# Attention over compressed blocks: high and low keys in one product of 64 columns, sums of two token tiles at once, score steps between the key features, two key banks kept in SBUF

## The chip, the cores and the metric

The kernel runs on one core of one Trainium2 chip. The core has five engines that share nothing but memory and semaphores: TensorE (PE in the rows; its weight loads are PEld), VectorE (DVE), ScalarE (ACT), GpSimd (POOL) and SyncE (SP), which issues the transfers. The metric is the device time of one execution in microseconds, the median of several runs. The inputs are float32; products are made either in float32 or with operands rounded to fp32r, a high part and a low part apart.

## The reference, cut to what matters

Two transformer blocks are computed for 512 tokens of width 1024. The change lies in the second one's mixer, which has 16 query heads of width 64 in 4 groups (heads of a group share keys), and three attentions that are gated and summed: over 31 compressed blocks of 32 tokens, over selected blocks, and over a window.

```python
q, kc, vc, ks, vs, kw, vw, gl = jnp.split(h @ w_in, cuts, axis=-1)
q = q.reshape(B, S, G, Hg, dk) * dk ** -0.5
gates = jax.nn.sigmoid(gl).reshape(B, S, G, Hg, 3)
k_cmp = _compress(kv(kc), pe_k, ck_w1, ck_w2)      # 31 compressed keys per group
v_cmp = _compress(kv(vc), pe_v, cv_w1, cv_w2)
...
p_cmp = masked_softmax(jnp.einsum('bghtd,bngd->bghtn', qg, k_cmp), cmp_end[None, :] <= t[:, None])
o_cmp = jnp.einsum('bghtn,bngd->btghd', p_cmp, v_cmp)
...
o = g_blk[..., 0:1] * o_cmp + g_blk[..., 1:2] * o_sel + g_blk[..., 2:3] * o_win
```

With 512 tokens all 8 selection blocks are taken, and the window covers all earlier tokens, so o_sel and o_win are two causal attentions with keys of their own.

## The kernel before

**Weights.** All projections go through one plan of weight tiles. SP loads them into a ring of six (`load_weights`, L322), ACT rounds each to its high part (`split_high`, L335, the copy is L344), POOL subtracts to get the low part (`split_low`, L347, L352), and PE makes three fp32r matmuls per block of 128 (`product`, L362: high times high, L365, and twice high times low, L366 and L367). ACT may round a tile only when PE has used the third tile before it, and SP may load one when POOL has made the low part of the sixth before it. Every engine runs its own list in the order of the code; engines meet at semaphores (`wait_ge`, `then_inc`).

**The stage around the change** starts at L2195. PE makes in turn: keys and values for compression, the 16 heads' queries (`nq`: rows 0 to 63 hold a head's high part, rows 64 to 127 its low part), the compression network, the token-major values (`values_of`; c=1 leaves them in PSUM banks 0 to 3, c=0 in banks 4 and 5), and four products with key features (`feature(k_at + i, i)`, 24 matmuls of 512 columns each, into banks 0 to 3). The attention over the compressed blocks is spread between these, for four token tiles t of 128 tokens:

- `block_scores(t)` (PE, L2287): for each of 16 heads two matmuls of 32 columns, one with the high and one with the low compressed keys `kcmp[0]`, `kcmp[1]`, into bank 6 + t % 2;
- `soften(t)` (DVE, L2456): mask added, row maximum, maximum subtracted; `block_exp(t)` (ACT, L2378); `norm_blocks(t)` (DVE, L2467): sum, reciprocal, gate, multiplied;
- `block_turn(t)` (PE, L2298): four transposes into the same bank; `block_copy(t)` (ACT, L2382) copies them to `cpT`;
- `block_values(t)` (PE, L2305): eight float32 products of 128 columns with `vcmp`, into banks 4 and 5 whatever t is; `finish(t)` (DVE, L2479) copies the sums to `oT`.

PE's order in the key features (L2346 to L2360): feature 0, turn 0, feature 1, values 0, scores 2, feature 2, turn 1, values 1, feature 3, scores 3, turn 2, values 2, turn 3, values 3.

**Keys.** When the four key features are in their banks, ACT copies 8 parts of 64 rows by 512 to `hT` (`key_high`), DVE makes the low parts (`key_low`), and SP copies each from rows 0 to 63 to rows 64 to 127 (L2561, four transfers per group, semaphore `k_twice[g]`).

**The next stage** ("pairs", L2566) runs 64 steps of two heads each over the four groups, the tiles and the two key sets: PE scores (L2600 to L2602), DVE maximum (L2688), ACT exponential (L2672), POOL reciprocal (L2720) and scaling (L2722), PE transposes (L2612), ACT and DVE high and low copies, PE values (L2627 to L2631), DVE sums into `oT`. PE makes the scores of the first step and then waits for `c_done`, that is for `finish(3)`; POOL's first step stands behind its last `split_low` of the stage before.

## Time and profile before

| what | value |
|---|---|
| median of 3 runs | 1810.1 us (1809.75 to 1811.23) |
| the profiled execution | 1811.46 us, its span 1809.7 us |
| PE busy | 1738.3 us, 96% of the span |
| DVE, ACT, POOL busy | 53%, 46%, 53% |
| mean granted TensorE clock | 0.981 |
| share of the last chain | PE 40%, DVE 5%, issue 2%, ACT 2%, POOL 1% |

The span runs from the first to the last instruction; 1.8 us of the execution lie around it. A granted clock of 1.00 is 2.4 GHz and 0.50 is 1.2 GHz. The stage of the change spans about 902 to 1078 us, the pairs 1078 to 1222 us. In a timeline row the first number is the start, the second the length; "x16" means that 16 instructions are merged; in square brackets stands the idle time of the engine before it and what ended that. Matmul ends are modelled, so the distance between two starts is the better measure of what one costs.

### The profile page before, as it was taken

Reading aid. Unit: us, or ns where it says so; the run is one execution under the profiler, and the core shown is the slowest. Engines: PE = TensorE matmul, PEld = TensorE weight load, DVE = VectorE, ACT = ScalarE, POOL = GpSimd, SP = SyncE. Lnnn points to the kernel's source line nnn. Section 1 sums busy time; section 2 is a strip of 40 time slices with the busy share of each in tenths; the row PEclk is TensorE's granted clock in tenths of the full one; section 3 lists DMA queues with packets and bytes.
Section 4 is the critical chain, followed back from the end, with each engine's and each line's share of the span. In section 5 each row is a group of like instructions: output and inputs, shape, how many; then the busy total and the mean of one; then the engine's idle time right before and its main releaser. Section 6 shows DMA issues by size and latency. Waiting matters only on the chain.

```text
span 1809.7 us, 27577 instructions
## 1 busy us (share of the span) xinstructions
PE 1738.3 (96%) x10430; PEld 1540.8 (85%) x10430; DVE 965.4 (53%) x1638; ACT 833.1 (46%) x1659; POOL 953.4 (53%) x697
## 2 busy tenths in 40 slices
PE   6999999999999999999899989999899999999998
PEld 4998887888878998999778978887788779989996
DVE  2246555353638742772346449994224388618842
ACT  4224543232335542553445238884434356516643
POOL 2454342344535764775346328992652358647852
PEclk9999999999999999999999979999999989999999
DMA  6232221123342332333235130012341223323331
GB/s 229 82 94 59 58 72 50 53 74 94 96 163 78 110 115 83 94 117 117 81 98 151 64 93 2 2 36 70 120 137 66 63 70 117 112 87 94 106 129 47
DMA packets 222901, 162.09 MB, mean 90 GB/s; under 512 B 9769, under 2 KB 197297, under 8 KB 222769
## 3 DMA queue, kind: packets, MB, share of 16 engines
q1 hardware_dynamic: 221712, 159.26, 28.8%
q8 instruction: 84, 1.38, 0.3%
q10 hardware_dynamic: 1056, 1.06, 0.2%
q14 instruction: 49, 0.39, 0.1%
HBM read 156.09 MB, written 2.11 MB: 87 GB/s over the span
## 4 chain that ended last, share of the span: by engine, by line
PE 40%; DVE 5%; issue 2%; ACT 2%; POOL 1%; DVEq 0%; ACTq 0%
PE psum L365 12%; PE psum L366 12%; PE psum L367 12%; DVE nprobL L2695 2%; DVE stat L2688 1%; PE psum L2612 1%; PE psum L2294 1%; POOL w_low L352 1%; PE psum L2628 0%; DVE oT L2704 0%; PE psum L2312 0%; PE psum L2627 0%; PE psum L449 0%; PE psum L2600 0%; ACT w_high L344 0%
## 5 line engine op out<-in xcount | busy, mean ns | idle before, releaser
L352 POOL TENSOR_TENSOR w_low<-ring,w_high 128x1024 fp32r<-128x1024 f32 (+2 forms) x223 | 483.4, 2172 | 633.0 <-ACT w_high L344 632.4
L365 PE MATMUL psum<-hT,w_high 128*128 128x512 f32 (+1 forms) x1072 | 377.5, 352 | 9.5 <-PEq L184 6.4
L344 ACT ACTIVATE w_high<-ring 128x1024 fp32r<-128x1024 f32 (+2 forms) x223 | 212.1, 954 | 375.3 <-PE psum L367 375.2
L366 PE MATMUL psum<-hL,w_high 128*128 128x512 f32 (+1 forms) x1072 | 371.4, 346 | 0.0
L367 PE MATMUL psum<-hT,w_low 128*128 128x512 f32 (+1 forms) x1072 | 371.1, 346 | 0.0
L365 PEld LDWEIGHTS psum<-hT,w_high 128*128 128x128 f32 x1072 | 206.9, 193 | 32.8 <-issue 6.6
L367 PEld LDWEIGHTS psum<-hT,w_low 128*128 128x128 f32 x1072 | 206.4, 193 | 24.9
L366 PEld LDWEIGHTS psum<-hL,w_high 128*128 128x128 f32 x1072 | 206.8, 193 | 21.8
L1784 POOL TENSOR_TENSOR w_low<-ffn_sums,w_high 128x512 fp32r<-128x512 f32 x120 | 169.1, 1423 | 51.1 <-ACT w_high L1779 50.8
L1784 POOL TENSOR_TENSOR w_low<-ring,w_high 128x512 fp32r<-128x512 f32 x120 | 155.1, 1294 | 60.7 <-ACT w_high L1779 53.9
L365 PE MATMUL psum<-ffn_th,w_high 128*128 128x256 f32 x640 | 181.6, 284 | 4.9 <-DVE ffn_g L2018 3.3
L367 PE MATMUL psum<-ffn_th,w_low 128*128 128x256 f32 x640 | 181.4, 283 | 0.0
L366 PE MATMUL psum<-ffn_tl,w_high 128*128 128x256 f32 x640 | 181.3, 283 | 0.0
L752 DVE TENSOR_TENSOR x<-x,psum 128x512 f32<-128x512 f32 x56 | 36.0, 683 | 230.2 <-PE psum L367 230.2
L365 PE MATMUL psum<-w_high,ffn_act 128*128 128x512 f32 x352 | 137.2, 390 | 0.0
L366 PE MATMUL psum<-w_low,ffn_act 128*128 128x512 f32 x352 | 137.0, 389 | 0.0
L367 PE MATMUL psum<-w_high,ffn_act 128*128 128x512 f32 x352 | 136.9, 389 | 0.0
L365 PEld LDWEIGHTS psum<-ffn_th,w_high 128*128 128x128 f32 x640 | 123.0, 192 | 5.5 <-DVE ffn_g L2018 3.7
L367 PEld LDWEIGHTS psum<-ffn_th,w_low 128*128 128x128 f32 x640 | 123.1, 192 | 0.0
L366 PEld LDWEIGHTS psum<-ffn_tl,w_high 128*128 128x128 f32 x640 | 123.0, 192 | 0.0
L365 PE MATMUL psum<-w_high,hT 128*128 128x256 f32 (+2 forms) x320 | 106.2, 332 | 3.6 <-POOL w_low L352 2.9
L1779 ACT ACTIVATE w_high<-ring 128x512 fp32r<-128x512 f32 x120 | 75.2, 630 | 73.2 <-PE psum L367 73.1
(436 smaller groups left out, 3775.8 us busy)
## 6 DMA issues: line engine op xcount, KB each, us to landing
ring<-in_w_in SPq DMA_DIRECT2D x58, 512.0 KB, 3.4
ring<-in_ffn_w_up SPq DMA_DIRECT2D x44, 512.0 KB, 3.8
ring<-in_w_gate SPq DMA_DIRECT2D x22, 512.0 KB, 3.7
ring<-in_w_up SPq DMA_DIRECT2D x22, 512.0 KB, 4.7
ring<-in_w_down SPq DMA_DIRECT2D x20, 512.0 KB, 3.7
ring<-in_ffn_w_down SPq DMA_DIRECT2D x20, 512.0 KB, 3.9
ring<-in_nsa_w_in SPq DMA_DIRECT2D x18, 512.0 KB, 3.5
ring<-in_ca_wkv SPq DMA_DIRECT2D x16, 512.0 KB, 3.6
```

What stands on the lines that cost most here:

```text
L344: nc.scalar.activation(tile_view(w_high, n, SPLIT), tile_view(ring, n, RING), ACT.Copy).then_inc(w_hi, 1)
L352: nc.gpsimd.tensor_tensor(tile_view(w_low, n, SPLIT), tile_view(ring, n, RING), tile_view(w_high, n, SPLIT), ALU.subtract).then_inc(w_lo, 1)
L365: nc.tensor.matmul(ps, lhsT=sh, rhs=mh, start=first, stop=False)
L366: nc.tensor.matmul(ps, lhsT=sh, rhs=ml_, start=False, stop=False)
L367: return nc.tensor.matmul(ps, lhsT=sl, rhs=mh, start=False, stop=last)
L752: return nc.vector.tensor_tensor(dst, dst, ps, ALU.add)
L1779: nc.scalar.activation(operand_place(w_high, r, j), self.source(r, name), ACT.Copy).then_inc(u_high, 1)
L1784: nc.gpsimd.tensor_tensor(operand_place(w_low, r, j), self.source(r, name), operand_place(w_high, r, j), ALU.subtract).then_inc(u_low, 1)
L2294: mm = nc.tensor.matmul(bank[6 + t % 2][:, 32 * h:32 * h + 32], lhsT=nq[:, h, q_tile(t)], rhs=kcmp[k][:, h // HPG, :], start=(k == 0), sto ...
L2612: mm = nc.tensor.transpose(bank[4 + v_ % 2][:, j * P:(j + 1) * P], nprob[:, v_ % 8, j * P:(j + 1) * P], ident)
L2688: nc.vector.tensor_reduce(np_peak[s % 2], psum[:, 2 * (s % 2):2 * (s % 2) + 2, 0:wd], AXX, ALU.max, negate=True).then_inc(p_peaked, 1)
L2695: nc.vector.tensor_tensor(nprobL[:, v_ % 4, 0:(t + 1) * P], bank[4 + v_ % 2][:, 0:(t + 1) * P], nprobT[:, v_ % 4, 0:(t + 1) * P], ALU.subt ...
```

## The change

Five things are different:

- **Side by side.** `kcmp` is one tile in which a group's high keys and low keys stand next to each other. `block_scores(t)` makes one matmul of 64 columns per head instead of two of 32, the two results land apart (two banks per tile, `scores_at`), and `soften(t)` has one more DVE step that adds them.
- **Two tiles at once.** `block_values(o)` takes both halves of `cpT`, so eight products of 256 columns serve two token tiles; there are two of them instead of four. They write four banks (2, 3, 6, 7), and the copies to `oT` are eight of 128x512: four on DVE for the first, then two on ACT and two on DVE for the second.
- **Order.** The key features go to banks 2 to 5. PE's order becomes: feature 0, turn 0, scores 2, feature 1, turn 1, scores 3, feature 2, turn 2, values 0, turn 3, feature 3, values 1. Before feature 2 PE waits until `soften(2)` is done, before turn 2 until `soften(3)` is done too.
- **Keys kept.** ACT copies banks 2 and 3 after features 0 and 1 to a new tile `nkraw` in SBUF (`keep_keys`, four copies of 64x512). All eight `key_high` come after feature 3 and before ACT's share of the last sums.
- **Low parts.** The four parts that come from `nkraw` are subtracted on POOL, the four from PSUM on DVE. POOL does its four before the last `split_low` of the stage. Each of SP's transfers of low parts waits for both engines. In the pairs, PE waits for `c_done` 8, ACT for POOL's four parts before step 2, and DVE once for `c_done` 8.

PE, from the third key feature to the first product of the pairs. L2301 and L2321 are the turns (before and now), L2312 and L2332 the sums, L365 to L367 a key feature, L2600 and L2622 scores of the pairs. Before, from the end of the last score product:

```order
L2294 MATMUL psum<-kcmp_10447,nq 128x32
L2301 MATMUL psum<-const,cscores 128x128 x4
L2312 MATMUL psum<-cpT,vcmp 128x128 x8
L2301 MATMUL psum<-const,cscores 128x128 x4
L2312 MATMUL psum<-cpT,vcmp 128x128 x8
L2588 UNCONDITIONAL_BRANCH
L2600 MATMUL psum<-hT,nq 128x128
```

Now, where "..." stands for the rest of the fourth key feature:

```order
L2321 MATMUL psum<-const,cscores 128x128 x4
L2332 MATMUL psum<-cpT,vcmp 128x256 x8
L2321 MATMUL psum<-const,cscores 128x128 x4
L365 MATMUL psum<-hT,w_high 128x512
...
L367 MATMUL psum<-hT,w_low 128x512
L2332 MATMUL psum<-cpT,vcmp 128x256 x8
L2610 UNCONDITIONAL_BRANCH
L2622 MATMUL psum<-hT,nq 128x128
```

Behind the last key feature stood one score step, two turns and two sums; now one sum of twice the columns stands there.

ACT, from the last key feature on. L344 rounds a weight tile, L372 copies keys (or sums), L2386 and L2403 copy turned weights, L2380 is an exponential. Before:

```order
L344 ACTIVATE w_high<-ring 128x1024
L372 ACTIVATE hT<-psum 64x512 x2
L2386 ACTIVATE cpT<-psum 128x512
L372 ACTIVATE hT<-psum 64x512 x2
L2380 ACTIVATE cscores<-cscores 128x512
L372 ACTIVATE hT<-psum 64x512 x4
L2386 ACTIVATE cpT<-psum 128x512
L344 ACTIVATE w_high<-ring 128x1024
```

Now:

```order
L2403 ACTIVATE cpT<-psum 128x512 x2
L372 ACTIVATE hT<-nkraw 64x512
L372 ACTIVATE hT<-psum 64x512
...
L372 ACTIVATE hT<-psum 64x512
L372 ACTIVATE oT<-psum 128x2x256 x2
L344 ACTIVATE w_high<-ring 128x1024
```

The copies of turned weights have moved ahead of the keys, and two copies of sums stand between the keys and the last weight tile.

POOL, where the stage ends and the pairs begin, before and then now:

```order
L352 TENSOR_TENSOR w_low<-ring,w_high 128x1024 x9
L2710 UNCONDITIONAL_BRANCH
L2712 MEMSET stat 128x2
L2720 TENSOR_TENSOR stat<-stat 128x2
```

```order
L352 TENSOR_TENSOR w_low<-ring,w_high 128x1024 x8
L2563 TENSOR_TENSOR hL<-nkraw,hT 64x512 x4
L352 TENSOR_TENSOR w_low<-ring,w_high 128x1024
L2737 UNCONDITIONAL_BRANCH
L2739 MEMSET stat 128x2
L2747 TENSOR_TENSOR stat<-stat 128x2
```

Four subtractions stand ahead of the last low part, which stands ahead of the first reciprocal of the pairs as before.

```diff
--- before.py
+++ after.py
@@ -2174,7 +2174,8 @@
         nv = nsa_tile("nv", [P, NT, 8, P], 49152, F32R)
-        kcmp = [nsa_tile(f"kcmp{i}", [P, NSA_G, 32], 65536 + 512 * i, F32R) for i in range(2)]
+        kcmp = nsa_tile("kcmp", [P, NSA_G, 2, 32], 65536, F32R)
         vcmp = nsa_tile("vcmp", [P, NSA_G, 256], 66560)
@@ -2187,6 +2188,8 @@
+        nkraw = nsa_tile("nkraw", [P, NSA_G, S], 87808)
         nprobL = nsa_tile("nprobL", [P, 4, S], 71424, F32R)
@@ -2208,6 +2211,7 @@
              "second", "kc_out", "v_out", "gated"))
+        k_low_g = sem("n_k_low_g", nsa)
         (c_scored, c_masked, c_exped, c_scaled, c_turned, c_copied, c_summed, c_done, c_chain, k_high, k_low) = (
@@ -2232,7 +2236,18 @@
-        key_parts = [(bank[2 * b + g // 2][HD * (g % 2):HD * (g % 2) + HD, :], 4 * b + g) for g in range(NSA_G) for b in range(2)]
+        key_parts = [(bank[4 + g // 2][HD * (g % 2):HD * (g % 2) + HD, :] if b else nkraw[0:HD, g, :], 4 * b + g)
+                     for g in range(NSA_G) for b in range(2)]
+        scores_at = (6, 0, 4, 0)
+        turned_at = (6, 7, 0, 1)
+        sums_at = (2, 3, 6, 7)
+        def block_sum(o, i):
+            return (oT[:, 2 * i:2 * i + 2, 2 * o * P:2 * (o + 1) * P],
+                    bank[sums_at[i]].rearrange("p (c n) -> p c n", n=2 * P))
@@ -2285,33 +2300,38 @@
             def block_scores(t):
+                b0 = scores_at[t]
                 if t == 0:
                     pe.wait_ge(kc_out, 1)
-                if t >= 2:
-                    pe.wait_ge(c_copied, t - 1)
+                elif t == 3:
+                    pe.wait_ge(c_masked, 2)
+                else:
+                    pe.wait_ge(nv_out, t * NT)
                 for h in range(NSA_H):
-                    for k in range(2):
-                        mm = nc.tensor.matmul(bank[6 + t % 2][:, 32 * h:32 * h + 32], lhsT=nq[:, h, q_tile(t)],
-                                              rhs=kcmp[k][:, h // HPG, :], start=(k == 0), stop=(k == 1))
+                    at_ = 64 * (h % 8)
+                    mm = nc.tensor.matmul(bank[b0 + h // 8][:, at_:at_ + 64], lhsT=nq[:, h, q_tile(t)],
+                                          rhs=kcmp[:, h // HPG, :, :].rearrange("p e n -> p (e n)"), start=True, stop=True)
                 mm.then_inc(c_scored, 1)
...
                 pe.wait_ge(c_scaled, t + 1)
+                if t == 2:
+                    pe.wait_ge(c_masked, NT)
                 for g in range(NSA_G):
-                    mm = nc.tensor.transpose(bank[6 + t % 2][:, g * P:(g + 1) * P],
+                    mm = nc.tensor.transpose(bank[turned_at[t]][:, g * P:(g + 1) * P],
                                              cscores[:, t % 2, 4 * g:4 * g + 4, :].rearrange("p h n -> p (h n)"), ident)
-            def block_values(t):
-                pe.wait_ge(c_copied, t + 1)
-                if t == 0:
-                    pe.wait_ge(nv_out, 2 * NT)
-                else:
-                    pe.wait_ge(c_done, t)
+            def block_values(o):
+                pe.wait_ge(c_copied, 2 * o + 2)
+                if o == 1:
+                    pe.wait_ge(c_done, 4)
                 for c in range(ND):
-                    mm = nc.tensor.matmul(bank[4 + c // 4][:, (c % 4) * P:(c % 4) * P + P],
+                    mm = nc.tensor.matmul(block_sum(o, c // 2)[1][:, c % 2, :].rearrange("p (t n) -> p t n", n=P),
                                           lhsT=vcmp[:, c // 2, (c % 2) * P:(c % 2) * P + P],
-                                          rhs=cpT[:, t % 2, (c // 2) * P:(c // 2) * P + P], start=True, stop=True)
+                                          rhs=cpT[:, :, (c // 2) * P:(c // 2) * P + P], start=True, stop=True)
                 mm.then_inc(c_summed, 1)
@@ -2344,20 +2364,17 @@
             for i in range(4):
-                pe.wait_ge(nv_out, i + 1)
-                feature(k_at + i, i)
-                if i == 0:
-                    block_turn(0)
-                if i == 1:
+                if i >= 2:
+                    pe.wait_ge(c_masked, 3)
+                feature(k_at + i, 2 + i)
+                if i < 2:
+                    block_turn(i)
+                    block_scores(2 + i)
+                if i == 2:
+                    block_turn(2)
                     block_values(0)
-                    block_scores(2)
-                if i == 2:
-                    block_turn(1)
-                    block_values(1)
-            block_scores(3)
-            for t in (2, 3):
-                block_turn(t)
-                block_values(t)
+                    block_turn(3)
+            block_values(1)
@@ -2381,9 +2398,14 @@
                 a.wait_ge(c_turned, t + 1)
-                if t >= 2:
-                    a.wait_ge(c_summed, t - 1)
-                nc.scalar.activation(cpT[:, t % 2, :], bank[6 + t % 2], ACT.Copy).then_inc(c_copied, 1)
+                if t == 2:
+                    a.wait_ge(c_summed, 1)
+                nc.scalar.activation(cpT[:, t % 2, :], bank[turned_at[t]], ACT.Copy).then_inc(c_copied, 1)
+            def keep_keys(i):
+                a.wait_ge(w_used, k_at + i + 1)
+                for j in range(2):
+                    copy(False, nkraw[0:HD, 2 * i + j, :], bank[2 + i][HD * j:HD * j + HD, :])
@@ -2408,26 +2430,26 @@
             nc.scalar.activation(ngate[:, :, :], ngate[:, :, :], ACT.Sigmoid).then_inc(gated, 1)
-            split_high(a, vb_at + 1 + SPLIT)
             block_exp(0)
             split_high(a, k_at + SPLIT)
+            keep_keys(0)
+            split_high(a, k_at + 1 + SPLIT)
+            block_copy(0)
             block_exp(1)
-            block_copy(0)
-            split_high(a, k_at + 1 + SPLIT)
-            block_exp(2)
+            keep_keys(1)
             split_high(a, k_at + 2 + SPLIT)
             block_copy(1)
+            block_exp(2)
+            block_exp(3)
             split_high(a, k_at + 3 + SPLIT)
+            block_copy(2)
+            block_copy(3)
             a.wait_ge(w_used, nsa_end)
-            for i in range(2):
+            for i in range(8):
                 key_high(i)
-            block_copy(2)
-            for i in range(2, 4):
-                key_high(i)
-            block_exp(3)
-            for i in range(4, 8):
-                key_high(i)
-            block_copy(3)
+            a.wait_ge(c_summed, 2)
+            for i in (0, 2):
+                copy(False, *block_sum(1, i)).then_inc(c_done, 1)
             split_high(a, nsa_end + SPLIT)
@@ -2459,7 +2481,10 @@
                 mask = const[:, C_CMP + 32 * t:C_CMP + 32 * t + 32].unsqueeze(1).to_broadcast([P, NSA_H, 32])
-                link(nc.vector.tensor_tensor(sv_, bank[6 + t % 2].rearrange("p (h n) -> p h n", n=32), mask, ALU.add))
+                b0 = scores_at[t]
+                src = psum[:, b0:b0 + 2, :].rearrange("p b (h e n) -> p (b h) e n", e=2, n=32)
+                link(nc.vector.tensor_tensor(sv_, src[:, :, 0, :], mask, ALU.add))
+                link(nc.vector.tensor_tensor(sv_, sv_, src[:, :, 1, :], ALU.add))
                 link(nc.vector.tensor_reduce(stat[:, 40:56], sv_, AXX, ALU.max))
@@ -2475,13 +2500,6 @@
-            def finish(t):
-                v.wait_ge(c_summed, t + 1)
-                for b in range(2):
-                    ins = nc.vector.tensor_copy(oT[:, 4 * b:4 * b + 4, q_tile(t)],
-                                                bank[4 + b].rearrange("p (c n) -> p c n", n=P))
-                ins.then_inc(c_done, 1)
@@ -2505,8 +2523,8 @@
             src = bank[7][:, 0:P].rearrange("p (g n) -> p g n", n=32)
-            link(nc.vector.tensor_copy(kcmp[0][:, :, :], src))
-            nc.vector.tensor_tensor(kcmp[1][:, :, :], src, kcmp[0][:, :, :], ALU.subtract)
+            link(nc.vector.tensor_copy(kcmp[:, :, 0, :], src))
+            nc.vector.tensor_tensor(kcmp[:, :, 1, :], src, kcmp[:, :, 0, :], ALU.subtract)
             for i in range(HPG):
@@ -2521,28 +2539,28 @@
             norm_blocks(0)
-            soften(1)
-            norm_blocks(1)
-            finish(0)
-            soften(2)
-            finish(1)
-            norm_blocks(2)
-            for i in range(2):
+            for t in range(1, NT):
+                soften(t)
+                norm_blocks(t)
+            v.wait_ge(c_summed, 1)
+            for i in range(4):
+                copy(True, *block_sum(0, i)).then_inc(c_done, 1)
+            for i in range(1, 8, 2):
                 key_low(i)
-            soften(3)
-            for i in range(2, 4):
-                key_low(i)
-            norm_blocks(3)
-            for i in range(4, 8):
-                key_low(i)
-            finish(2)
-            finish(3)
+            v.wait_ge(c_summed, 2)
+            for i in (1, 3):
+                copy(True, *block_sum(1, i)).then_inc(c_done, 1)
...
             nc.gpsimd.memset(vcmp[:, :, :], 0.0).then_inc(zeroed, 1)
+            split_low(g, k_at + 3 + SPLIT)
+            for i in range(0, 8, 2):
+                src, kb = key_parts[i]
+                g.wait_ge(k_high, i + 1)
+                nc.gpsimd.tensor_tensor(hL[0:HD, kb, :], src, hT[0:HD, kb, :], ALU.subtract).then_inc(k_low_g, 1)
             split_low(g, nsa_end + SPLIT)
@@ -2555,8 +2573,12 @@
             for g in range(NSA_G):
-                for part_, done in ((hT, k_high), (hL, k_low)):
-                    sp.wait_ge(done, 2 * g + 2)
+                for part_ in (hT, hL):
+                    if part_ is hT:
+                        sp.wait_ge(k_high, 2 * g + 2)
+                    else:
+                        sp.wait_ge(k_low_g, g + 1)
+                        sp.wait_ge(k_low, g + 1)
                     for kb in (g, 4 + g):
@@ -2633,7 +2655,7 @@
-            pe.wait_ge(c_done, NT)
+            pe.wait_ge(c_done, 8)
             for s in range(n_np + 4):
@@ -2663,6 +2685,9 @@
                     a.wait_ge(p_peaked, s + 1)
+                    if s == 2:
+                        a.wait_ge(k_low_g, NSA_G)
                     for i in range(2):
@@ -2699,6 +2724,8 @@
                     v.wait_ge(p_summed, 2 * o + 2)
+                    if o == 0:
+                        v.wait_ge(c_done, 8)
                     dst = oT[HD * hp:HD * hp + HD, 2 * g:2 * g + 2, q_tile(t)]
```

## Rows read from the trace of the kernel before

**Rows 1.** Windows by stretch: PE, PEld, DVE, ACT, POOL busy us (instructions), PEclk, DMA share, GB/s.

```profile
1022.10:1028.80 6.70, 6.70 (x22) 5.64 (x22) 5.76 (x12) 0.78 (x2) 2.36 (x1) 0.50 0.48 157
1028.90:1042.50 13.60, 13.60 (x85) 12.02 (x85) 2.84 (x7) 1.54 (x2) 2.40 (x1) 1.00 0.00 1
1042.60:1049.30 6.70, 6.70 (x19) 5.44 (x19) 2.07 (x3) 1.58 (x2) 1.90 (x1) 0.50 0.00 0
...
1073.30:1086.80 13.50, 11.95 (x54) 11.61 (x55) 5.53 (x13) 4.39 (x21) 7.32 (x13) 0.50 0.70 207
1087.00:1222.00 135.00, 129.83 (x978) 117.97 (x977) 124.39 (x242) 114.95 (x369) 121.70 (x188) 1.00 0.04 13
```

**Rows 2.** Timeline of PE, 1010 to 1078 us: start, length, instruction, idle before.

```profile
1010.15 3.64 PE L2294 MATMUL psum<-kcmp,nq 128*128 128x32 f32 x32
1013.64 0.37 PE L365 MATMUL psum<-w_high,hT 128*128 128x256 f32 x1
...
1019.48 4.50 PE L2294 MATMUL psum<-kcmp,nq 128*128 128x32 f32 x32
1023.82 0.77 PE L365 MATMUL psum<-hT,w_high 128*128 128x512 f32 x1
...
1031.76 0.60 PE L2301 MATMUL psum<-const,cscores 128*128 128x128 f32 x4
1032.11 0.48 PE L365 MATMUL psum<-hT,w_high 128*128 128x512 f32 x1
...
1039.39 4.14 PE L2294 MATMUL psum<-kcmp,nq 128*128 128x32 f32 x32
1043.37 0.77 PE L365 MATMUL psum<-hT,w_high 128*128 128x512 f32 x1
...
1053.02 2.05 PE L2312 MATMUL psum<-cpT,vcmp 128*128 128x128 f32 x16 [0.69 <-ACT cpT L2386]
1054.82 0.48 PE L365 MATMUL psum<-hT,w_high 128*128 128x512 f32 x1
...
1060.38 4.44 PE L2294 MATMUL psum<-kcmp,nq 128*128 128x32 f32 x32
...
1074.56 3.75 PE L2312 MATMUL psum<-cpT,vcmp 128*128 128x128 f32 x16 [3.40 <-DVE oT L2482]
1077.96 0.45 PE L2600 MATMUL psum<-hT,nq 128*128 128x128 f32 x1
```

**Rows 3.** Timeline of PE in the pairs: fp32r products of 128 columns at full clock.

```profile
1113.33 0.28 PE L2601 MATMUL psum<-hL,nq 128*128 128x128 f32 x1
1113.44 0.28 PE L2602 MATMUL psum<-const_r 128*128 128x128 f32 x1
```

**Rows 4.** Groups by line and shape: float32 products of an earlier stage, 300 to 400 us.

```profile
L1200 PE MATMUL psum<-mqkT 128*128 128x256 f32 x4 | 1.3, 404 | 0.0
L1200 PE MATMUL psum<-mqkT 128*128 128x128 f32 x4 | 0.9, 300 | 0.0
```

**Rows 5.** Timeline of DVE in the score steps of tile 1.

```profile
1025.58 0.68 DVE L2462 TENSOR_TENSOR cscores<-psum,const 128x512 f32<-128x512 f32 x1
...
1028.40 0.69 DVE L2470 TENSOR_REDUCE stat<-cscores 128x16 f32<-128x512 f32 x1 [0.69 <-ACT cscores L2380]
...
1029.90 0.69 DVE L2476 TENSOR_TENSOR cscores<-cscores,stat 128x512 f32<-128x512 f32 x1
```

**Rows 6.** Timeline of ACT behind the last key feature.

```profile
1060.58 1.07 ACT L372 ACTIVATE hT<-psum 64x512 fp32r<-64x512 f32 x2 [6.67 <-PE psum L367]
...
1071.70 1.05 ACT L344 ACTIVATE w_high<-ring 128x1024 fp32r<-128x1024 f32 x1
```

**Rows 7.** Timeline of POOL: the last weight tile and the first step of the pairs.

```profile
1072.82 2.34 POOL L352 TENSOR_TENSOR w_low<-ring,w_high 128x1024 fp32r<-128x1024 f32 x1 [16.46 <-ACT w_high L344]
...
1080.96 0.70 POOL L2720 TENSOR_TENSOR stat<-stat 128x2 f32<-128x2 f32 x1 [5.76 <-ACT nprob L2672]
```

**Rows 8.** Transfers, 1061 to 1075 us: count, KB each, median us from issue to landing.

```profile
hT<-hT SPq DMA_DIRECT2D x8, 128.0 KB, 2.3
```

## The prediction

> **What bounds the kernel now.** I read the page first: PE is busy for 96% of the span and carries 40% of the last chain, the next engine 5%. So most time is PE's, but a busy PE is not a fast one. The windows by stretch [rows 1] say more: in the stage of the change PE is busy all through 1022.1 to 1028.8 us and 1042.6 to 1049.3 us, at a granted clock of 0.50, the lower of its two levels, while the 13.6 us between them have 1.00. From 1073.3 to 1086.8 us it is 0.50 again. In the pairs PE, DVE and POOL are busy for 130, 124 and 122 of 135 us: three engines near their limit, so a later start of the pairs moves the end, and no engine has room to make it up. Next comes PE's timeline [rows 2]. What the reader is to see is where the low stretches begin: score products start at 1019.48 and the clock is down at 1022.1; they start at 1039.39 and it is down at 1042.6. 32 matmuls of 32 columns keep PE busy and give it next to nothing to multiply. The last piece is the tail: the last key feature ends at 1060.38, yet POOL's first step of the pairs starts at 1080.96 [rows 7]. Those 20.58 us hold one score step, two turns and two sums, the last of which waited 3.40 us for DVE's copies of the one before.
>
> So there are two places with something to win: from 1010.15 to 1060.38 (PE alone sets the pace, 50.23 us), and from there to POOL's first step (20.58 us).
>
> **Side by side.** At full clock the first score step takes 1013.64 - 1010.15 = 3.49 us for 32 matmuls, 0.109 us each [rows 2]. What does one of 64 columns cost? No row has 64. One of 128 columns takes 0.11 us from start to start [rows 3], as much as one of 32: up to there the weight load, not the columns, sets the distance. So 16 x 0.109 = 1.75 us per tile. The steps before the key features and between them took 3.49, 4.34 (1019.48 to 1023.82) and 3.98 us (1039.39 to 1043.37), the latter two partly at the low clock: 11.8 us. Now four such steps stand there, 7.0 us.
>
> **The clock.** Feature 0 took 1031.76 - 1023.82 = 7.94 us, feature 3, at full clock, 1060.38 - 1054.82 = 5.56 us [rows 2]. Feature 2 with its turn and the wait behind it took 1053.02 - 1043.37 = 9.65 us. With half as many matmuls, each of twice the columns, and other products on both sides, I expect both low stretches to go: four features at 5.56 = 22.2 us. Support comes from the first score step: its 3.49 us between dense products brought no fall of the clock, though its matmuls were as thin, and the new steps take half as long. The Trainium skill speaks against this ("TensorE: Matmul & The Clock Gate", sections "HAM oscillation" and "Why this matters for your kernels"): it puts a fall of the clock down to stretches in which TensorE idles. By that rule the score products, which leave no idle time, would not be to blame, and the two stretches would stay; the trace does not agree, since PE was busy for all of the time before both.
>
> **Two tiles at once.** Float32 products cost by the column: an earlier stage has them at 300 ns for 128 and 404 ns for 256 columns, 104 ns more for 128 more columns [rows 4]. A sum of today is 1.80 us (1053.02 to 1054.82) for 16 instructions of 128 columns, 0.11 each; at 256 columns they are 0.11 + 0.104 = 0.21, so one new sum is 3.4 us, as much as the two that it replaces. The lower end, were only the weight load to count, is 1.9 us. I take 3.4, since the rows are of the same kind of product. The gain of this part is not on PE: the last sum no longer waits for a copy.
>
> **Spread among the key features.** PE from 1010.15 to the end of feature 3: values 5.84 (1013.64 to 1019.48), scores 7.0, features 22.2, four turns of 0.35 (1031.76 to 1032.11) = 1.4, one sum 3.4, and what it must wait. PE waits for `soften(3)` before turn 2. Counted from 1010.15, feature 1 ends at 1032.7 and feature 2 at 1040.4. Behind feature 1 ACT has, after 0.2 of signalling: two kept keys 1.07, a weight tile 1.05 [rows 6], then a copy and the exponential of tile 2, of 512 columns like a key, so 0.535 each: 1036.1. Then DVE: `norm_blocks(2)`, 1029.90 + 0.69 - 1028.40 = 2.19 us [rows 5], and `soften(3)`, now four steps of 0.68 and some 0.03 between them, 2.85 us; with 0.1 for each signal 1041.4. PE waits 1.0 us. Ends: 0 if ACT's items are shorter by a quarter each, 2.5 if each is longer by half. For turn 0, `norm_blocks(0)` ended before 1025.58, when DVE began the next tile [rows 5]; all ahead of it is now one score step earlier, 1.74, so 1023.9, and PE is there at 1025.1. For turn 1, ACT has the same items behind feature 0, so DVE is done at 1025.1 + 3.4 + 2.3 = 1030.8, and PE comes at 1032.7. Both are hidden, by 1.2 and 1.9 us. The extra DVE step and the kept keys cost nothing but what is in this wait. Sum: 5.84 + 7.0 + 22.2 + 1.4 + 3.4 + 1.0 = 40.8 us against 50.23, a gain of **9.4 us**. Feature 3 ends 9.4 us earlier, at 1051.0.
>
> **The tail.** From there (T) to POOL's first step two paths lead. Copies: ACT starts at T + 0.2 [rows 6]; eight keys at 0.535 = 4.3, so T + 4.5 (the sum of PE, T + 3.6, is done); two copies of sums, of 512 columns too, 1.1; the weight tile 1.05; T + 6.65. POOL's low part 2.34 us behind it [rows 7], the memset and signals 0.3: T + 9.3. Keys: the second key is high at T + 1.3; both its low parts (DVE 0.7, a step of 512 columns [rows 5]; POOL 1.2, half of the 2.34 us for 1024 columns [rows 7], taken for 64 rows too) are there by T + 2.1; SP issues four transfers one behind the other; if that takes until T + 3.9, the last lands 2.3 us later [rows 8]: T + 6.2. From the first score product of the pairs to POOL's step it took 1080.96 - 1077.96 = 3.0 us [rows 2, 7] at the low clock; at full clock the six products of the step are 0.6 us shorter: T + 8.6. So the first path is last by 0.7 us, and the tail is 9.3 instead of 20.58 us: **11.3 us** gained. POOL's four subtractions end at T + 5.9 and are hidden behind ACT's weight tile; without that cover they would cost their own 4.8 us. The added waits (PE and DVE for `c_done`, ACT for POOL's parts) are satisfied by T + 6.6, when DVE has made its four low parts and two copies. What is late next is POOL itself, since it had no idle time once the pairs ran.
>
> PE idles from T + 3.6 to T + 6.2, so the clock will be low again when the pairs begin, as it was from 1073.3 to 1086.8, of which 5.9 us lay behind POOL's first step. It may last longer here. Bounds: 0 and 3 us (one more stretch of 6.8 us of which PE sets the pace for less than all); I take 0.4, near the lower end, because POOL sets the pace of the first steps.
>
> **Sum.** 9.4 + 11.3 - 0.4 = 20.3 us. The profiled execution took 1811.46 us, 1.36 above the median: 1791.2 us for such an execution, **1789.8 us** for the median.
>
> **Rivals.**
> (a) The low clock stays between the key features: one stretch (6.8 us at half rate, 3.4 us lost) gives 1793.2 us, both give 1796.6 us. Against it: the first score step. For it: the skill's rule above, and that turns and scores now stand side by side.
> (b) POOL is slow with 64 rows: at the 2.34 us of a whole weight tile [rows 7], four take 9.4 us, POOL's last low part starts at T + 10.3 instead of T + 6.8, 3.5 us later: 1793.3 us.
> (c) More is gained: the wait before turn 2 vanishes (1.0) and the sum costs 1.9 us (1.5): 1787.3 us.
> (d) It does not do what it says: a matmul of 64 columns costs twice one of 32. Then the four steps take 14.0 us, and the gain falls by 7.0: 1796.8 us. [rows 3] speak against it.
> (e) Slower: after PE's idle time in the tail the first steps of the pairs are too thin to bring the clock back. In half-clock PE, not POOL, sets the pace; each us at 0.50 costs up to 0.5. Before, it came back after 13.5 us. It would have to last 41 us longer to eat the 20.3 us; through the first two groups of the pairs (68 us) it would cost up to 34 - 3 = 31 us, so 1821 us. Against it: 1.00 throughout 1087 to 1222 [rows 1], thin first steps of the later groups included.
>
> **How the numbers follow.** The forecast has 0.50 (1788 to 1791.5 by itself), (a) 0.17 with one stretch and 0.06 with both, (b) 0.07, (c) 0.15, (d) 0.02, (e) 0.03. The range goes from 1786.5, a little under (c), to 1796, over (a) with one stretch and (b) together with a longer low start of the pairs; it leaves out both stretches, (d) and (e), about 0.12. 0.2% is 3.6 us, about what a measurement of this kernel can tell from no change. All but (e) are faster by more: faster 0.96, the same 0.01, slower 0.03.
>
> **What would show it.** In the changed kernel's trace: score steps of 16 matmuls in 1.75 us; granted clock 1.00 from 1010 us to the end of the last key feature; a wait of about 1 us before turn 2; 16 instructions at 0.21 us in a sum; the last key feature ending near 1051 us; POOL's first reciprocal 9.3 us later, right behind its last weight tile; a pair stage as long as before. The prediction is wrong if the clock falls in the key features, if the first scores of the pairs start much later than T + 6.2, or if the pairs take longer than the 144 us of before (1078 to 1222).

## The result and the profile after

| what | before | after |
|---|---|---|
| median | 1809.9 us (1809.13 to 1811.23) | 1792.33 us (1791.61 to 1792.66) |
| ratio of the two, 95% interval | | 0.9900 [0.9888, 0.9911] |
| profiled execution, its span | 1811.46, 1809.7 us | 1791.61, 1789.8 us |
| mean granted TensorE clock | 0.981 | 0.989 |
| first score product to the end of the span | 799.5 us | 779.2 us |
| share of the last chain | PE 40%, DVE 5% | PE 39%, DVE 5% |

The changed kernel is 17.6 us faster by the medians and 19.85 us by the two profiled executions. The forecast for the median was 1789.8 us, in a range (1786.5 to 1796) that holds 1792.33; the narrower band that the prediction gave to its main course, 1788 to 1791.5 us, does not.

PE's timeline of the changed kernel in the stage of the change; L2312 are score products, L2321 turns, L2332 sums, L365 the start of a feature, L2622 the pairs (start, length, instruction, idle before it):

```profile
1010.64 1.87 PE L2312 MATMUL psum<-kcmp,nq 128*128 128x64 f32 x16
1012.34 0.36 PE L365 MATMUL psum<-w_high,hT 128*128 128x256 f32 x1
...
1025.81 1.95 PE L2312 MATMUL psum<-kcmp,nq 128*128 128x64 f32 x16
1027.60 0.48 PE L365 MATMUL psum<-hT,w_high 128*128 128x512 f32 x1
...
1041.89 0.63 PE L2321 MATMUL psum<-const,cscores 128*128 128x128 f32 x4 [0.86 <-DVE cscores L2489]
1042.35 3.62 PE L2332 MATMUL psum<-cpT,vcmp 128*128 128x256 f32 x16
1046.81 0.66 PE L2321 MATMUL psum<-const,cscores 128*128 128x128 f32 x4 [0.83 <-DVE cscores L2501]
...
1052.76 3.61 PE L2332 MATMUL psum<-cpT,vcmp 128*128 128x256 f32 x16
1058.30 0.33 PE L2622 MATMUL psum<-hT,nq 128*128 128x128 f32 x1 [1.93 <-DMA hL<-hL]
```

A score step takes 1.70 us from start to start (1010.64 to 1012.34) where it took 3.49 to 4.34 [rows 2]; a wait stands ahead of each of the last two turns; behind the last feature (1052.76) there is one sum, and the pairs begin 5.54 us later, where it took 17.58.

The windows of the changed kernel by stretch, with the columns of [rows 1]:

```profile
1010.60:1052.80 42.20, 40.50 (x243) 35.45 (x242) 26.80 (x48) 12.03 (x17) 11.91 (x5) 1.00 0.10 34
1060.20:1067.00 6.80, 6.66 (x31) 6.12 (x31) 2.95 (x8) 4.60 (x23) 6.40 (x11) 0.50 0.89 224
1067.20:1202.20 135.00, 130.05 (x977) 117.73 (x975) 124.63 (x243) 114.66 (x367) 123.06 (x189) 1.00 0.08 25
```

The clock is 1.00 all through the stage, where before two stretches of 6.7 us had 0.50; at the start of the pairs it is low for 6.8 us instead of 13.5. The pairs are close to what they were.

POOL's timeline where the stage ends, and its first steps of the pairs:

```profile
1053.66 4.96 POOL L2563 TENSOR_TENSOR hL<-nkraw,hT 64x512 fp32r<-64x512 f32 x4 [7.88 <-ACT hT L372]
1059.61 2.37 POOL L352 TENSOR_TENSOR w_low<-ring,w_high 128x1024 fp32r<-128x1024 f32 x1 [0.99 <-ACT w_high L344]
...
1062.10 0.71 POOL L2747 TENSOR_TENSOR stat<-stat 128x2 f32<-128x2 f32 x1
1062.91 0.89 POOL L2749 TENSOR_SCALAR nprob<-nprob,stat,ngate 128x128 f32<-128x128 f32 x2
1063.76 0.72 POOL L2747 TENSOR_TENSOR stat<-stat 128x2 f32<-128x2 f32 x1
```

From 1059.61 on POOL has no idle time, and goes from step to step in 1.66 us. In the trace of before it waited 5.76 us for an exponential ahead of its first step [rows 7].

**A yardstick.** The first score product stands at 1010.2 to 1014.1 us, by what happened ahead of it in each execution, so the runs below are compared by distances from the first score product: to POOL's first reciprocal of the pairs, to its second last one (number 63 of 64, near the end of the pairs), and to the end of the span.

| trace | first score | POOL's first | POOL's 63rd | end |
|---|---|---|---|---|
| before | 1010.15 | 70.81 | 205.21 | 799.5 |
| before, again (e2) | 1014.13 | 68.38 | 201.81 | 796.2 |
| changed kernel | 1010.64 | 51.46 | 184.93 | 779.2 |
| changed kernel, again (e1) | 1011.45 | 51.46 | 184.90 | 779.2 |
| changed kernel, third (e10) | 1013.24 | 51.46 | 184.71 | 779.0 |
| e3, thin products | 1011.67 | 64.55 | 197.95 | 792.9 |
| e4, POOL later | 1012.98 | 53.30 | 186.78 | 779.9 |
| e5, scores in one place | 1012.01 | 65.22 | 198.66 | 792.9 |
| e6, other form | 1011.04 | 51.46 | 184.87 | 779.2 |
| e7, low parts on DVE | 1011.83 | 51.48 | 185.03 | 779.4 |
| e8, tile later | 1010.86 | 50.41 | 183.85 | 778.9 |
| e9, exponential earlier | 1012.32 | 49.41 | 183.31 | 779.1 |
| e11, sums of one tile | 1012.26 | 51.48 | 184.92 | 776.5 |
| e12, tile between | 1013.63 | 51.20 | 186.50 | 782.3 |

### The profile page after: what moved, and what is told of

It is laid out like the page before. It is cut to its first block, busy times and chain, and to the rows that moved or that the text cites. A ratio compares the mean times of both kernels' runs of the same rounds, so it can differ in the third digit from the quotient of the medians.

```text
span 1789.8 us, 27394 instructions
## 1 busy us (share of the span) xinstructions
PE 1719.5 (96%) x10334; PEld 1521.6 (85%) x10334; DVE 960.8 (54%) x1636; ACT 837.0 (47%) x1665; POOL 961.6 (54%) x701
## 4 chain that ended last, share of the span: by engine, by line
PE 39%; DVE 5%; issue 3%; ACT 2%; POOL 1%; DVEq 0%; ACTq 0%
PE psum L365 12%; PE psum L367 12%; PE psum L366 12%; DVE nprobL L2720 2%; DVE stat L2713 1%; PE psum L2634 1%; POOL w_low L352 1%; DVE oT L2731 0%; PE psum L2650 0%; PE psum L2649 0%; ACT w_high L344 0%; PE psum L449 0%; PE psum L2312 0%; DVE x L438 0%; PE psum L2622 0%
## 5 line engine op out<-in xcount | busy, mean ns | idle before, releaser
L365 PE MATMUL psum<-hT,w_high 128*128 128x512 f32 (+1 forms) x1072 | 375.2, 350 | 9.5 <-PEq L184 6.4
L344 ACT ACTIVATE w_high<-ring 128x1024 fp32r<-128x1024 f32 (+2 forms) x223 | 212.2, 955 | 367.5 <-PE psum L367 367.4
L367 PE MATMUL psum<-hT,w_low 128*128 128x512 f32 (+1 forms) x1072 | 369.2, 344 | 0.0
L365 PEld LDWEIGHTS psum<-hT,w_high 128*128 128x128 f32 x1072 | 205.6, 192 | 32.3 <-issue 6.6
L367 PEld LDWEIGHTS psum<-hT,w_low 128*128 128x128 f32 x1072 | 205.1, 191 | 24.5
L365 PE MATMUL psum<-ffn_th,w_high 128*128 128x256 f32 x640 | 181.6, 284 | 4.9 <-DVE ffn_g L2018 3.3
L367 PE MATMUL psum<-ffn_th,w_low 128*128 128x256 f32 x640 | 181.4, 283 | 0.0
L365 PE MATMUL psum<-w_high,ffn_act 128*128 128x512 f32 x352 | 137.2, 390 | 0.0
L367 PE MATMUL psum<-w_high,ffn_act 128*128 128x512 f32 x352 | 136.9, 389 | 0.0
L365 PEld LDWEIGHTS psum<-ffn_th,w_high 128*128 128x128 f32 x640 | 123.0, 192 | 5.5 <-DVE ffn_g L2018 3.8
L367 PEld LDWEIGHTS psum<-ffn_th,w_low 128*128 128x128 f32 x640 | 123.1, 192 | 0.0
L365 PE MATMUL psum<-w_high,hT 128*128 128x256 f32 (+2 forms) x320 | 106.3, 332 | 3.6 <-POOL w_low L352 2.9
```

What stands on the lines that cost most here:

```text
L344: nc.scalar.activation(tile_view(w_high, n, SPLIT), tile_view(ring, n, RING), ACT.Copy).then_inc(w_hi, 1)
L365: nc.tensor.matmul(ps, lhsT=sh, rhs=mh, start=first, stop=False)
L367: return nc.tensor.matmul(ps, lhsT=sl, rhs=mh, start=False, stop=last)
```

## The experiments

### Both kernels once more

> The changed kernel as it is, for a second trace and a narrow interval. The two profiled executions differ by 19.9 us, the medians by 17.6. Theory A (the execution of before that was profiled was one of the slower ones, 1811.46 against 1809.92, and that of the changed kernel one of the faster ones, 1791.61 against 1792.33): this trace shows the same stage, a median near 1792, and the rest of the difference is one more stretch at the low clock, somewhere, in most executions (mean clock 0.986 instead of 0.989). Theory B (the stage itself varies): the last key feature ends at another time than 42.1 us after the first score product.

> The kernel before, for a second trace. Theory A: its low stretches stand where they stood (from 1022, 1042, 1063 and 1073 us), since the score products and the idle tail cause them. Theory B: they are elsewhere, and the first trace was one case of several.

The changed kernel again: median 1793.09 us against 1811.23, ratio 0.9902 [0.9883, 0.992]; its stage repeats to the hundredth (first score product at 1011.45, POOL's first reciprocal 51.46 us later, end 779.2). The third trace of the changed kernel (e10, below) has the same distances but starts the stage at 1013.24 us, 2.6 us later than the first: its clock is 0.90 over the first 50 us, where the first has 1.00. So the lower mean clock of that execution (0.985 instead of 0.989) comes from low stretches ahead of the stage. Before does not repeat. Its second trace:

```profile
1026.10:1032.90 6.80, 6.80 (x22) 5.74 (x22) 5.86 (x12) 0.77 (x2) 2.36 (x1) 0.50 0.45 154
1046.60:1050.00 3.40, 3.40 (x12) 2.82 (x11) 2.07 (x3) 0.33 (x1) 0.00 (x0) 0.50 0.00 0
1073.90:1080.70 6.80, 4.59 (x22) 4.62 (x22) 2.83 (x6) 0.38 (x1) 2.38 (x2) 0.50 0.84 225
1084.10:1087.50 3.40, 3.40 (x19) 3.25 (x18) 2.02 (x6) 2.72 (x15) 3.19 (x8) 0.51 0.24 73
```

The low clock is there behind the same score products, but the second stretch is 3.4 us long instead of 6.7 (and so is the third, from 1067.1 us, instead of 6.8 from 1063.0), and at the pairs 10.2 us are low in two pieces instead of 13.5 in one. So this execution is 3.4 us shorter from the first score product to the end than the execution on which the prediction's sum was made. Its later start (1014.13) hid that in the total, 1812.05 us. Against this trace the changed kernel gains 17.0 us, against the first one 20.3.

### Two products of 32 columns for one of 64

```diff
-                    mm = nc.tensor.matmul(bank[b0 + h // 8][:, at_:at_ + 64], lhsT=nq[:, h, q_tile(t)],
-                                          rhs=kcmp[:, h // HPG, :, :].rearrange("p e n -> p (e n)"), start=True, stop=True)
+                    for e in range(2):
+                        mm = nc.tensor.matmul(bank[b0 + h // 8][:, at_ + 32 * e:at_ + 32 * e + 32], lhsT=nq[:, h, q_tile(t)],
+                                              rhs=kcmp[:, h // HPG, e, :], start=True, stop=True)
```

> The changed kernel with two score products of 32 columns for each of 64; all else as it is, the same numbers at the same places. Theory A (thin products cost their weight load and bring the clock down): 16 more per tile at 0.109 us, 7.0 us for four tiles, and low stretches return among the key features, 2 to 7 us more: 9 to 14 us above the changed kernel. Rival (the low stretches had nothing to do with the width of the products): 7 us and the clock stays at 1.00 until the tail.

Median 1806.01 us, ratio 0.9966 [0.9955, 0.9977]: 12.9 us over the changed kernel of e1. PE and the windows of this run:

```profile
1011.67 3.64 PE L2313 MATMUL psum<-kcmp,nq 128*128 128x32 f32 x32
1021.00 4.32 PE L2313 MATMUL psum<-kcmp,nq 128*128 128x32 f32 x32
...
1066.90 3.40 PE L2333 MATMUL psum<-cpT,vcmp 128*128 128x256 f32 x15
```

```profile
1011.70:1023.80 12.10, 12.10 (x108) 12.10 (x106) 5.26 (x11) 2.75 (x3) 2.84 (x2) 1.00 0.07 28
1023.80:1030.60 6.80, 6.80 (x21) 5.64 (x21) 5.30 (x11) 0.00 (x0) 1.84 (x1) 0.50 0.45 154
1037.50:1040.80 3.30, 3.30 (x9) 2.53 (x8) 3.12 (x7) 0.00 (x0) 0.56 (x1) 0.50 0.02 5
1047.80:1054.50 6.70, 6.70 (x19) 5.50 (x20) 5.66 (x11) 0.67 (x2) 1.33 (x1) 0.50 0.00 0
```

The last feature ends 55.2 us after the first score product instead of 42.1. The four score steps take 15.4 us instead of 7.0 (8.4 more, of which 7.0 at full clock), three features at a partly low clock 8.1, 7.2 and 8.2 us instead of some 5.6 (6.6 more), and the two waits (1.7) are gone, since PE is late itself. Undoing this edit alone takes back two thirds of the gain, about half of it by the instructions themselves and half by the clock. PE was busy for every bit of the 12.1 us ahead of the first fall. The Trainium skill's rule ("TensorE: Matmul & The Clock Gate", section "HAM oscillation"), by which idle gaps bring the clock down, does not cover this case: here twice as many products of half the width did, with no gap. Whether their number or their width counts is not told apart.

### The old order put back

Scores of tile 3 and turns 2 and 3 stand behind the last key feature again, and the first sum behind feature 1:

```diff
-                    block_scores(2 + i)
-                if i == 2:
-                    block_turn(2)
+                if i == 0:
+                    block_scores(2)
+                if i == 1:
                     block_values(0)
-                    block_turn(3)
+            block_scores(3)
+            block_turn(2)
+            block_turn(3)
             block_values(1)
```

> The changed kernel with the old place of the late steps: scores of tile 3, turns 2 and 3 and both waits for DVE stand behind the last key feature again, the first sum behind feature 1. Theory A (the place, not the sums of two tiles, gives the gain of the tail): the last key feature ends some 4.2 us earlier counted from the first score product, but the keys' copies on ACT stand behind the chain scores 1.7, softening 2.9, exponential 0.7, norm 2.2, turn 0.4, copy 0.6, so POOL's first step comes some 9 us later behind it: 4 to 6 us above the changed kernel, about 1798. Rival (the tail was short because the sum no longer waits for a copy, and the place matters little): within 1.5 us of the changed kernel.

Median 1805.55 us, ratio 0.9971 [0.9958, 0.9983]; from the first score product to the end 792.9 us, 13.7 more than the changed kernel, where 4 to 6 had been expected. PE in this run:

```profile
1037.57 5.41 PE L2332 MATMUL psum<-cpT,vcmp 128*128 128x256 f32 x16 [2.42 <-ACT cpT L2405]
...
1053.74 1.87 PE L2312 MATMUL psum<-kcmp,nq 128*128 128x64 f32 x16
...
1058.65 1.09 PE L2321 MATMUL psum<-const,cscores 128*128 128x128 f32 x4 [3.04 <-DVE cscores L2491]
...
1063.56 1.12 PE L2321 MATMUL psum<-const,cscores 128*128 128x128 f32 x4 [3.82 <-DVE cscores L2503]
...
1066.04 6.58 PE L2332 MATMUL psum<-cpT,vcmp 128*128 128x256 f32 x16 [1.37 <-DVE oT L371]
```

```profile
1058.40:1072.00 13.60, 8.16 (x22) 6.26 (x23) 9.41 (x14) 6.99 (x12) 7.29 (x5) 0.50 0.29 67
```

The chain of scores, exponential, turn, copy and sum stands bare behind the last feature: PE waits three times, 8.2 us together, and the clock is 0.50 for 13.6 us of it, so that the last sum takes 6.2 us instead of 3.6. POOL's first step comes 23.5 us behind the last feature instead of 9.34. The last feature ends 41.7 us after the first score product, only 0.4 us earlier than in the changed kernel where 4.2 had been expected: the first sum, moved too, waits 2.42 us for a copy and takes 5.05 us instead of 3.6, partly at a low clock (0.50 over the 3 us from 1038 us). So the 13.7 us are the price of the whole order, some 3.8 of them from the place of the first sum, and the rest from behind the last feature; the expectation had left out that wait and the clock. Undoing either part costs about 13 us, more than half of the whole each, because both bring the low clock back.

### Sums of one tile

```diff
-                    mm = nc.tensor.matmul(block_sum(o, c // 2)[1][:, c % 2, :].rearrange("p (t n) -> p t n", n=P),
-                                          lhsT=vcmp[:, c // 2, (c % 2) * P:(c % 2) * P + P],
-                                          rhs=cpT[:, :, (c // 2) * P:(c // 2) * P + P], start=True, stop=True)
+                    for t in range(2):
+                        mm = nc.tensor.matmul(block_sum(o, c // 2)[1][:, c % 2, t * P:(t + 1) * P],
+                                              lhsT=vcmp[:, c // 2, (c % 2) * P:(c % 2) * P + P],
+                                              rhs=cpT[:, t, (c // 2) * P:(c // 2) * P + P], start=True, stop=True)
```

> The changed kernel with each product over two token tiles (256 columns, float32) written as two products of one tile (128 columns) with the same values as weights: 16 products for a sum instead of 8, everything else and every place unchanged. Theory: a float32 product of 256 columns is two instructions of 0.214 us, one of 128 columns two of 0.107 us, so that both sums keep their 3.4 us each and the change's gain does not come from the wider products but from where the sums stand: from the first score product to the end 779.0 to 779.8 us, median within 0.7 us of the changed kernel's 1792 to 1794. Rival (each new weight costs its own time, as in the key products): each sum over 4 us, the first score product to the end 780.5 us or more, 1.5 us or more slower, and perhaps a low clock that comes back as with the thin products (then 5 us or more).

Median 1792.85 us, ratio 0.9912 [0.9895, 0.9928]. A sum takes 3.7 us instead of 3.6:

```profile
1043.97 3.74 PE L2333 MATMUL psum<-cpT,vcmp 128*128 128x128 f32 x32
```

POOL's first reciprocal is 51.48 us behind the first score product, as before the edit. Products of two tiles at once bring nothing by their width. What is left of this part is that the last sum no longer stands behind a copy of the one before, for which PE waited 3.40 us before; that was not undone by itself. The end comes at 776.5 us, under the expected 779.0: not by the edit, but because a low stretch 450 us later was not there in this execution. The same stretch of work in the changed kernel and in this run:

```profile
1460.00:1470.00 10.00, 7.97 (x54) 7.97 (x55) 8.86 (x15) 4.47 (x8) 6.46 (x5) 0.83 0.35 105
```

```profile
1461.60:1471.60 10.00, 9.09 (x75) 9.09 (x76) 9.13 (x18) 6.70 (x13) 8.80 (x7) 1.00 0.36 107
```

The distance to the end moves by 2.7 us with it. Differences below that are read from POOL's steps instead.

### Is it POOL that the pairs start with?

POOL gets one more operation ahead of its first step (its result isn't used; `vcmp` is no longer read by then):

```diff
+            g.wait_ge(c_summed, 2)
+            nc.gpsimd.tensor_tensor(vcmp[:, :, :], vcmp[:, :, :], vcmp[:, :, :], ALU.subtract)
```

> The changed kernel with one more POOL subtraction of 128x1024 (2.35 us, of a tile that is no longer read) between its last low part and its first step of the pairs. Theory A of the prediction (POOL's path through the last weight tile sets when the pairs get going): 2.3 to 2.4 us more. Rival (PE and DVE set it, POOL has slack): POOL's first step came 18.9 us earlier, but all that followed 20.1 us earlier, so some 1.2 us are slack and only 1.1 to 1.2 us are added.

Median 1794.84 us, against 1793.09 of the changed kernel beside it. The added operation took 1.89 us, not the 2.35 expected. POOL and PE:

```profile
1064.27 1.89 POOL L2566 TENSOR_TENSOR vcmp<-vcmp 128x1024 f32<-128x1024 f32 x1
...
1066.28 0.71 POOL L2749 TENSOR_TENSOR stat<-stat 128x2 f32<-128x2 f32 x1
```

```profile
1067.60 0.48 PE L2636 MATMUL psum<-const,nprob 128*128 128x128 f32 x1 [1.64 <-POOL nprob L2751]
```

The first step is 1.84 us later, PE now waits for POOL, and the 63rd step is 1.85 us later as well: the delay passes through the whole of the pairs. The end of the span is only 0.7 us later, and I first took that for slack of POOL; but this is again an execution without the later low stretch. 290 us behind the first score product it was 3.4 us behind the changed kernel (1.5 more than at the end of the pairs; the last experiment comes back to them), and the missing stretch gave 2.7 back.

The next run rests on that misreading. All eight low parts of the keys go to DVE:

```diff
-            for i in range(1, 8, 2):
+            for i in range(8):
                 key_low(i)
...
-            for i in range(0, 8, 2):
-                src, kb = key_parts[i]
-                g.wait_ge(k_high, i + 1)
-                nc.gpsimd.tensor_tensor(hL[0:HD, kb, :], src, hT[0:HD, kb, :], ALU.subtract).then_inc(k_low_g, 1)
```

> The changed kernel with all eight low parts of the keys on DVE, none on POOL. Theory A (PE and DVE set the start of the pairs, POOL has 1.1 us of slack): DVE has four more steps of 0.7 us but waits for ACT between them now, so it ends its two copies of sums about 1.2 us later, and the second step of the pairs and the end come 0.9 to 1.2 us later. Rival (POOL's path decides): no difference or a gain, since POOL's weight tile is only ready when ACT is.

Median 1791.24 us, ratio 0.9893 [0.9878, 0.9907]. DVE ends its copies 0.65 us later (its first maximum is at T + 7.34 instead of T + 6.69, T being the end of the last feature), POOL keeps its first step and its 63rd is 0.1 us later. A delay of DVE of this size is hidden, one of POOL isn't: POOL sets the start. It also shows that the change's split of the low parts over two engines brings nothing here, since ACT's eight copies set their pace.

The reverse: POOL's and ACT's weight tile is taken out of the end of their lists.

```diff
             for i in range(8):
+                if i == 4:
+                    split_high(a, nsa_end + SPLIT)
                 key_high(i)
...
             for i in range(0, 8, 2):
+                if i == 4:
+                    split_low(g, nsa_end + SPLIT)
```

> The changed kernel, with the last weight tile of the tail taken out of the end of two lists: ScalarE rounds it behind the fourth of the eight key parts instead of behind the copies of the sums, GpSimd makes its low part between its second and its third key part instead of behind the fourth. Nothing is added or left out; GpSimd's idle time of 0.99 us ahead of the tile goes, and ScalarE's last four key parts and its copies of the second sum come 1.05 us later. Theory (GpSimd sets the pace of the first steps over pairs, so what reaches its first step reaches the end of the pairs): GpSimd's first reciprocal comes 50.4 to 50.9 us after the first score product instead of 51.46, and the last addition to the output sums of the pairs 193.0 to 193.6 instead of 193.99. Rival (TensorE, VectorE and the copies of the sums set it): no earlier than 193.9, and later by up to 1 us, since the copies end later. The end of the span and the median say little at this size: the low clock stretches behind the pairs moved them by more than this between equal kernels. Median 1791.5 to 1794.5 us.

Median 1797.65 us (1791.8 to 1797.75) against 1811.56 of before. POOL and PE:

```profile
1064.83 0.70 POOL L2749 TENSOR_TENSOR stat<-stat 128x2 f32<-128x2 f32 x1 [0.73 <-ACT nprob L2699]
```

```profile
1063.56 0.47 PE L2624 MATMUL psum<-hT,nq 128*128 128x128 f32 x1 [1.35 <-DVE oT L371]
```

POOL was ready 1.0 us earlier but then waited 0.73 for an exponential, so its first step came only 0.26 earlier; PE waited 1.35 us for the copies of the sums instead of 0.40, and the clock was low for 10.2 us instead of 6.8. The 63rd step came 1.6 us later, and so did the last addition to the sums (195.59 us behind the first score product instead of 193.99), more than the rival's 1 us. My theory fell here: POOL sets the start, but another path stands close behind it. In the changed kernel the exponentials that POOL's first step needs end at T + 7.9, and here, with the copies later, at T + 8.9; POOL itself was free at T + 9.3 and is now at T + 8.3. That leaves some 1.2 us to spare in the changed kernel. The 1.8 us that the pairs lost behind POOL's first step are not explained by the longer low clock alone: e4 had the same 10.2 us of it and lost nothing there (133.48 us from POOL's first to its 63rd step, here 135.30).

### The wait that the prediction did not have

DVE's small multiplication for the last tile, in the changed kernel, and what POOL does beside it:

```profile
1043.16 0.25 DVE L2496 RECIPROCAL stat<-stat 128x16 f32<-128x16 f32 x1
1043.45 2.36 DVE L2497 TENSOR_SCALAR stat<-stat,const 128x16 f32<-128x16 f32 x1
```

```profile
1043.43 2.35 POOL L352 TENSOR_TENSOR w_low<-ring,w_high 128x1024 fp32r<-128x1024 f32 x1 [5.43 <-ACT w_high L344]
```

It ends with POOL's operation, which started 0.02 us ahead of it. The other three tiles have it too, with less left of POOL's operation. In tile 1 the reciprocal ran beside POOL at its usual length, while the multiplication behind it ended with POOL's operation there too (1030.31 and 1030.29):

```profile
1029.70 0.25 DVE L2496 RECIPROCAL stat<-stat 128x16 f32<-128x16 f32 x1
1029.98 0.33 DVE L2497 TENSOR_SCALAR stat<-stat,const 128x16 f32<-128x16 f32 x1
```

```profile
1027.88 2.41 POOL L352 TENSOR_TENSOR w_low<-ring,w_high 128x1024 fp32r<-128x1024 f32 x1 [5.00 <-ACT w_high L344]
```

The trace of before had shown it, in tile 0, where the multiplication ended 0.03 us behind POOL's operation; the prediction took its cost from tile 1, where POOL stood still:

```profile
1023.85 0.87 DVE L2472 TENSOR_SCALAR stat<-stat,const 128x16 f32<-128x16 f32 x1
```

```profile
1022.33 2.36 POOL L352 TENSOR_TENSOR w_low<-ring,w_high 128x1024 fp32r<-128x1024 f32 x1 [0.53 <-ACT w_high L344]
```

Is it the form of the instruction?

```diff
-                link(nc.vector.tensor_scalar(stat[:, 80:96], stat[:, 80:96],
-                                             const[:, C_VALID + t:C_VALID + t + 1], None, ALU.mult))
+                link(nc.vector.tensor_tensor(stat[:, 80:96], stat[:, 80:96],
+                                             const[:, C_VALID + t:C_VALID + t + 1].to_broadcast([P, 16]), ALU.mult))
```

> The changed kernel with the multiplication by the column of valid rows in the norm step written as a tensor_tensor with a broadcast instead of a tensor_scalar. In the changed kernel's trace that instruction took 2.36 us for tile 3 (0.33 us for tiles 1 and 2) while POOL ran a weight tile of 2.35 us, and PE waited 0.83 us behind it. Theory A (that form of DVE instruction cannot start or finish while POOL works on SBUF, the others can): it takes 0.2 us for all tiles, and the last key feature ends 0.8 us earlier. Rival (any small DVE instruction at that moment would be held up): 2.3 us again, no gain.

```profile
1043.85 2.36 DVE L2497 TENSOR_TENSOR stat<-stat,const 128x16 f32<-128x16 f32 x1
```

Median 1792.23 us; the same 2.36 us, the same wait of 0.83. Then its neighbour: ACT rounds the weight tile behind the copies of the turned scores, so that POOL works on it later.

```diff
-            split_high(a, k_at + 3 + SPLIT)
             block_copy(2)
             block_copy(3)
+            split_high(a, k_at + 3 + SPLIT)
```

> The changed kernel, with one ScalarE instruction moved: the high part of the weight tile that ScalarE writes at 1042.31 us, and that GpSimd's 2.35 us operation at 1043.43 waits for, is written behind the two copies of the turned scores instead of ahead of them. GpSimd's operation then starts near 1049 and no longer stands beside VectorE's normalization of tile 3. Theory (VectorE's small instruction is held until GpSimd's operation ends, and so the turn of tile 3 waits 0.83 us): VectorE's multiplication by the column of valid entries, 2.36 us at 1043.45, takes about 0.3 us, TensorE's wait of 0.83 us ahead of the turn of tile 3 is gone, the wait of 0.86 us ahead of the turn of tile 2 stays, and from the first score product to the span's end it is about 778.4 us instead of 779.2; the median comes out 0 to 1 us lower. Rival (the 2.36 us are the instruction's own in that place, or come from the transfers): still over 2 us long, and the wait of 0.83 us stays.

```profile
1043.67 0.23 DVE L2497 TENSOR_SCALAR stat<-stat,const 128x16 f32<-128x16 f32 x1
```

```profile
1046.03 0.60 PE L2321 MATMUL psum<-const,cscores 128*128 128x128 f32 x4
```

0.23 us instead of 2.36, the wait is gone, and POOL's steps are 1.05 us earlier from the first to the 63rd (1.08). So DVE was held by POOL. The end of the span came only 0.2 us earlier, not the 0.8 expected; the last run shows where it went. The Trainium skill says why an engine is held ("SBUF — State Buffer", section "SBUF: two separate sides"): the two engines share a pair of ports, and the one that starts first has it for its whole instruction. VectorE needs the pair when it reads two inputs from SBUF while GpSimd reads from it too, and also in a mode that uses both ports, which the page says `tensor_scalar` can enter. The traces agree for both forms: each was held (2.36 us), the reciprocal and the sum over a row, with one input in SBUF, were not (0.25 and 0.69 us). Which of the two reasons holds the `tensor_scalar` no run here tells. So the opening section's "share nothing but memory and semaphores" is too simple for these two engines.

Last, both waits at once: ACT's exponential of tile 2 comes ahead of the copy and the weight tile that stood before it, and the second sum is copied ahead of the last two key parts.

```diff
             keep_keys(1)
-            split_high(a, k_at + 2 + SPLIT)
+            block_exp(2)
             block_copy(1)
-            block_exp(2)
+            split_high(a, k_at + 2 + SPLIT)
             block_exp(3)
-            split_high(a, k_at + 3 + SPLIT)
             block_copy(2)
             block_copy(3)
+            split_high(a, k_at + 3 + SPLIT)
```

> The move of e8, and three more orders. ScalarE's exponential of tile 2 comes ahead of the weight tile and the copy that stood before it, so that it starts near 1033.8 us + its wait instead of 1036.04, and those of tiles 2 and 3 and the normalizations behind them end 1 to 2 us earlier. In the tail the second sum is copied before the last group of keys, by ScalarE and VectorE both. Theory: both waits of TensorE between the scores and the sums (0.86 and 0.83 us) vanish, 1.7 us; the copies of the second sum end about 1 us earlier, worth 0 to 0.5 us, since the run with all low parts on VectorE showed 0.65 us there to cost nothing. From the first score product to the end about 777.3 us (776.9 to 777.6) instead of 779.2; median 1.5 to 2 us below that of the changed kernel in the same call, near 1790.8 us. Rival (the first steps over pairs are bound by the keys, not by the score phase, or the low clock comes back): 779 us or more, and no difference between the medians.

> The changed kernel once more, to stand beside e8 and e9 on the same chip: 1792 to 1793.5 us, 779.2 us from the first score product to the end.

```profile
1042.55 0.60 PE L2321 MATMUL psum<-const,cscores 128*128 128x128 f32 x4
...
1046.44 0.60 PE L2321 MATMUL psum<-const,cscores 128*128 128x128 f32 x4
```

Both waits are gone, POOL's first step is 2.05 us earlier, its 63rd 1.6. The hold shows here the other way round as well: POOL's operation started while DVE ran the last multiplication of `norm_blocks(2)`, with two inputs in SBUF (from 1038.29 us for 0.69), and took 2.83 us instead of 2.35 to 2.41:

```profile
1038.42 2.83 POOL L352 TENSOR_TENSOR w_low<-ring,w_high 128x1024 fp32r<-128x1024 f32 x1 [6.45 <-ACT w_high L344]
```

Yet from the first score product to the end it is 779.1 us, not the 777.3 expected, and the medians side by side are 1793.56 us (e9), 1792.2 (e8) and 1794.01 (the changed kernel, where 1792 to 1793.5 had been expected): no difference that can be told. The traces show where it went. The 16 us behind the pairs in which TensorE waits for weight tiles, in the changed kernel, in e8 and in e9, each at the same distance from the first score product:

```profile
1258.00:1274.00 16.00, 10.37 (x73) 10.20 (x74) 2.56 (x5) 5.80 (x9) 8.64 (x5) 0.89 0.36 110
```

```profile
1258.20:1274.20 16.00, 11.43 (x75) 11.25 (x76) 2.56 (x5) 5.80 (x9) 7.83 (x5) 0.79 0.39 130
```

```profile
1259.70:1275.70 16.00, 11.80 (x74) 11.59 (x74) 2.56 (x5) 5.80 (x9) 7.58 (x4) 0.79 0.35 110
```

A clock of 0.79 instead of 0.89 over 16 us is 3.2 us more at half rate, up to 1.6 us of work. The 1.08 and 1.6 us that both kernels had at the end of the pairs were down to 0.2 and 0.1 at the end of the span. It is not the earlier arrival that makes this stretch longer, as these two traces alone would suggest. Two that arrive later, e4 and e12 (POOL's 63rd step 1.85 and 1.57 us later), have 0.79 there too and lost 1.5 us each behind the pairs. So has e3; e1, e5, e6, e7, e10 and e11 have 0.89. The same 16 us of work in e4:

```profile
1262.30:1278.30 16.00, 10.43 (x61) 10.25 (x62) 2.14 (x4) 4.79 (x9) 8.24 (x4) 0.79 0.31 96
```

What decides between 0.79 and 0.89 stays open. No kernel of these beats the changed one by more than its measurement can tell.

## Why the prediction was right, and where it was off

**What bounds the kernel, and the two places to win at:** right. 19.35 us are gained between the first score product and POOL's first step of the pairs, 20.28 at its 63rd, and about 20.3 at the end of the span. Of the five differences, the kept keys (`nkraw`) were not undone by themselves; the split of the low parts brought nothing.

**Scores.** 16 products at 0.106 to 0.112 us, four steps 6.98 us, forecast 7.0. Rival (d) is out. **The clock:** 1.00 throughout the stage, features 5.54 to 5.71 us; rival (a) is out, and the run with thin products brought the low clock back by that edit alone.

**Sums.** 3.6 us where 3.4 were taken, 0.214 us from one instruction to the next as forecast; rival (c)'s 1.9 us is out.

**Waits.** Before turn 2: 0.86 us, forecast 1.0. Before turn 3: 0.83 us, forecast none. This is the term that failed: the sum has none for `norm_blocks(3)`. At the 2.19 us of [rows 5], taken from a tile in which POOL stood still, it would have been hidden behind the first sum; the multiplication in it took 2.1 us more beside POOL, and 0.83 of them came out. With it and some 0.6 us more in the turns, the sum and one feature, less 0.14 in the first wait, the first part took 42.12 us, not 40.8, and gained 8.1 us, not 9.4.

**Tail.** 9.34 us, forecast 9.3. ACT's eight keys, two copies and weight tile end at T + 6.8 (forecast 6.65), POOL's four parts take 1.24 us each (1.2; rival (b) is out) and are hidden, PE's first product of the pairs is at T + 5.5 (6.2). Gained 11.2 us, forecast 11.3. POOL's own start as the last thing holds as well, by some 1.2 us, but what stands behind it was taken wrongly. The prediction had 0.7 us to spare over the path through the keys (T + 9.3 and T + 8.6) and took the copies of the sums as done in time; e12 showed the path through the copies to be the next one.

**The clock at the start of the pairs.** A loss of 0.4 us was taken. It turned into a gain: the low stretch fell from 13.5 to 6.8 us (rival (e) is out), and the pairs from POOL's first to its 63rd step went from 134.40 to 133.47 us, 0.9 less. The second trace of before has 133.43 us there, so this gain belongs to one execution of before. It made up for most of the wait: 8.1 + 11.2 + 0.9 is 20.3 with rounding (POOL's 63rd step: 20.28), the sum of the forecast. That it was met to the tenth is luck: two errors cancel.

**Where the 2.5 us of the median are.** The sum was carried from one execution to the median. From the first score product to the end the profiled execution gained just the 20.3 us, and came out at 1791.61 us for a forecast of 1791.2 (its stage began 0.5 us later). The prediction then took 1.4 us off for the median; but this execution lies 0.7 us under its own median, and a typical one can start the stage later (e10: 2.6 us). And that execution of before had its low stretches at full length, and the second trace, with 3.4 us less of distance, gives a gain of 17.0 us. The medians moved by 17.6 us, and by 18.1 and 14.8 us in two later comparisons: the typical execution of before seems to lie nearer to the second trace, of which there is only one. A gain that is partly a removed low clock is worth what that clock cost on average, and one trace gives one draw of it.

## What to carry to other kernels

Count the thin products, not only their time: with 32 columns each they cost as much as with 64 and held the clock down for the dense work behind them, which doubled the price. What follows a dependent chain (scores, exponential, turn, sum) should be spread among independent products early enough that none of it is left for the end of the stage. A small VectorE instruction on SBUF can be held until the GpSimd operation beside it ends (0.23 us became 2.36 here): look at what stands beside it in the new order before costing it from the old one.

## What the runs showed of the hardware that was not expected

- A 128x16 VectorE multiplication took 2.36 us beside a GpSimd operation of 2.35 us, in two forms, and 0.23 us without it; a GpSimd operation took 2.83 us instead of 2.35 to 2.41 when a VectorE instruction with two SBUF inputs was running at its start.
- The granted clock falls without any idle time of TensorE: after 12.1 us in which it was busy throughout, in the run with 32-column products. The same score work in 64-column products brought no fall.
- Low stretches of the clock differ from one execution to the next of the same kernel: three of 6.7 to 6.8 us or one of 6.8 and two of 3.4 in the score phase of before, and one behind the pairs that was missing in two of twelve traces (e4, e11) and moves the end by 2.7 us, and one nearer to the pairs that is some 3.4 us longer in five of the twelve (e3, e4, e8, e9, e12). This is more than the edits of e6 to e9 are worth, which is why those were read from distances inside the trace.
